# Opening stage of a decoder-layer kernel: constants in two batches, row sums taken from the rows as loaded, six token groups, and two weight tiles interleaved with the transposes

## The chip, the cores and the metric

The kernel is one launch on one core of a Trainium2 chip. The metric is the device time of that core in microseconds (us), and less is better. All arithmetic is fp32: the large products are made of TensorE's fp32r products of high and low parts, the small ones are plain fp32.

## The reference

One layer of a decoder trunk runs over 576 tokens: a prompt of 512 and eight samples of 8 tokens each. The change touches the opening of the layer, up to the first weight tiles of the first feed-forward block:

```
def rmsnorm(x, g):
    y = x * lax.rsqrt(jnp.mean(x * x, axis=-1, keepdims=True) + EPS)
    return y * g

def swiglu_ffn(x, norm_g, w_gu, w_down):
    h = rmsnorm(x, norm_g)
    g, u = jnp.split(h @ w_gu, 2, axis=-1)
    return (jax.nn.silu(g) * u) @ w_down

x = x + 0.5 * swiglu_ffn(x, norm_ffn1, ffn1_w_gu, ffn1_w_down)   # x: (576, 1024), w_gu: (1024, 5632)
...
```

After it come a projection `w_in`, a convolution branch, latent attention over the prompt and over a paged cache for the samples, a gated merge, `w_out` and a second feed-forward block of the same shape. None of these is changed.

## The kernel before, in words

**Layout.** Activations are held transposed, channels on the 128 partitions and the 576 tokens along the free axis: `xT` is eight channel tiles of 128 x 576. A product writes a unit, two PSUM banks with 288 tokens each (`halves`, `HALF`). The text counts `t` for channel tiles of x (0 to 7) and `n` for column tiles of weights; the first block has 44 of them before its down projection, gate and up in turn.

**Three products for one.** Every fp32 weight tile is split in a high part (`split_hi`, L351, ACT, a rounding copy into one of `HIS = 2` buffers) and a low part (`split_lo`, L358, POOL, four instructions, written over the raw tile in one of `RAWS = 4` buffers). `product` (L367) then does hi x hi, hi x lo and lo x hi for each of 8 channel tiles and 2 halves: 48 matmuls of 288 columns for one column tile.

**Norm.** The gain is folded into x (`x_hi`, `x_lo`); the factor 1/rms per token (`rstd`) is applied when a unit is read from PSUM (`scaled`, L1353). So the products need no norm, and only the first reading of a unit does.

**The opening, engine by engine.** ACT's queue issues 13 DMAs of constants, in this order: seven rows of gains, the convolution's taps, the identity matrix, the causal mask, the rotary table and two rows of gains broadcast (L642 to L648). All raise one semaphore, `const_in`. SP issues five DMAs for x (L440, L441) and eight for the first four weight tiles (`load_chunk`, L338), and then waits with each further tile for `w_used`. PE waits for all 13 constants (L933), transposes the gains and the taps into the columns `cols`, waits for x and transposes it, 5 transposes for each of 8 channel tiles (four of 128 tokens, one of 64), with room in PSUM for four channel tiles (L947). Only then come column tile 0, the sums, and column tiles 1, 2, 3. For each channel tile DVE copies the transposed tile to `xT` in two instructions (L1346, L1347), forms `x_lo` (L1326) and adds the squares to `sumsq` (L1333); ACT squares the tile (L656) and forms `x_hi` (L657). `sums` (L961) is three fp32 matmuls of ones with `sumsq`; DVE (`inverse`, L1335) and ACT (`rstd_root`, L659) make `rstd` of them.

**What sets the order.** Every engine has its own program, written out by hand, and counts on semaphores. What matters here of ACT's order, from `up_phase` (L692): split of column tile 2, root, split of tile 3, `hidden` for the first pair (SiLU, then the high part of the result), and only then the splits of tiles 4 and 5. `split_hi` of tile n waits for the end of tile n - 2 (`w_used`). `chunk` (L951) on PE waits for the low part of its tile. DVE's `hidden` (L1357) reads two units, multiplies by ACT's SiLU and forms the low part.

## Time and profile before

| | |
|---|---|
| Median of 3 runs | 1736.98 us (1735.47 to 1738.48) |
| Profiled execution, own time | 1737.28 us |
| Its span in the profile | 1735.5 us |
| PE busy | 1634.6 us, 94% of the span |
| DVE, POOL, ACT busy | 746.7, 608.5, 530.8 us |
| From the start to the first large matmul | 30.2 us |

A span is the time from the first to the last instruction of the trace; the execution's own time is 1.8 us longer. PE is TensorE's matmuls, PEld its loads of the stationary operand, DVE is VectorE, ACT ScalarE, POOL GpSimd, SP the queue that issues most DMAs. A name with q (SPq, ACTq) is that engine's sequencer. "issue" is a wait for nothing that the profile shows.

### The profile page before, as it was taken

How to read it: one execution, taken by the hardware profiler on the slowest of the kernel's cores; microseconds unless marked ns; L12 is line 12 of the kernel's file. 1: busy time of each engine (PE TensorE's matmuls, PEld its weight loads, DVE VectorE, ACT ScalarE, POOL GpSimd, SP SyncE). 2: the span in 40 equal slices, each digit the busy share in tenths (PEclk: the TensorE clock that was granted, in tenths of full speed). 3: DMA queues.
4: the chain of work that ended last, by engine and by line, in shares of the span. 5: the costliest groups of instructions: out<-in, count | busy, mean ns of one | idle time of the engine just before them, and what ended most of it. 6: DMA issues, size and time to landing. Idle time of an engine off the chain costs nothing.

```text
span 1735.5 us, 31195 instructions
## 1 busy us (share of the span) xinstructions
PE 1634.6 (94%) x11545; PEld 1546.3 (89%) x11545; DVE 746.7 (43%) x1147; ACT 530.8 (31%) x915; POOL 608.5 (35%) x693
## 2 busy tenths in 40 slices
PE   5999999999899999787999999978999999999998
PEld 4999999999899998375988888867999999999997
DVE  5322222121269856663666666666543222221001
ACT  3222222222121232242544444434233222222110
POOL 2455555544345544100000000002655555454441
PEclk9999999999999999897999999998999999999999
DMA  4222223322223421001212122210222222223221
GB/s 125 74 85 85 83 75 88 101 83 79 60 74 95 118 61 54 0 1 52 56 46 58 53 57 54 57 36 25 85 85 73 85 85 80 77 85 101 84 83 55
DMA packets 230060, 122.05 MB, mean 70 GB/s; under 512 B 28223, under 2 KB 226983, under 8 KB 229972
## 3 DMA queue, kind: packets, MB, share of 16 engines
q1 hardware_dynamic: 229150, 120.56, 24.4%
q8 instruction: 43, 0.70, 0.2%
q10 hardware_dynamic: 830, 0.48, 0.1%
q14 instruction: 37, 0.30, 0.1%
HBM read 117.79 MB, written 3.58 MB: 70 GB/s over the span
## 4 chain that ended last, share of the span: by engine, by line
PE 83%; DVE 6%; issue 4%; ACT 3%; POOL 2%; SPq 1%; DMA 1%; ACTq 0%; DVEq 0%; POOLq 0%
PE ps L377 61%; PE ps L1250 11%; PE ps L1197 3%; POOL w_lobuf L363 2%; PE ps L1104 1%; PE ps L1183 1%; PE ps L1071 1%; ACT prob L800 1%; PE ps L1078 1%; PE ps L1223 1%; DMA gqk<-in_q_head_norm 1%; DVE s_buf L1695 1%; DVE y L1410 1%; SPq L499 1%; SPq L500 0%
## 5 line engine op out<-in xcount | busy, mean ns | idle before, releaser
L363 POOL TENSOR_TENSOR w_lobuf<-w_rawbuf,w_hibuf 128x256 fp32r<-128x256 f32 (+1 forms) x664 | 583.9, 911 | 662.6 <-ACT w_hibuf L356 662.6
L377 PE MATMUL ps<-x_hi,w_hibuf 128*128 128x288 f32 x1888 | 408.9, 298 | 8.6 <-POOL w_lobuf L363 3.1
L377 PE MATMUL ps<-x_hi,w_lobuf 128*128 128x288 f32 x1888 | 407.4, 297 | 0.0
L377 PE MATMUL ps<-x_lo,w_hibuf 128*128 128x288 f32 x1888 | 407.0, 297 | 0.0
L356 ACT ACTIVATE w_hibuf<-w_rawbuf 128x1024 fp32r<-128x1024 f32 (+1 forms) x166 | 185.3, 1116 | 679.1 <-PE ps L377 679.1
L377 PEld LDWEIGHTS ps<-x_hi,w_hibuf 128*128 128x128 f32 x1888 | 305.1, 189 | 11.4 <-issue 4.5
L377 PEld LDWEIGHTS ps<-x_hi,w_lobuf 128*128 128x128 f32 x1888 | 305.1, 189 | 0.4
L377 PEld LDWEIGHTS ps<-x_lo,w_hibuf 128*128 128x128 f32 x1888 | 305.0, 189 | 0.4
L377 PE MATMUL ps<-a_lo,w_hibuf 128*128 128x288 f32 x704 | 151.2, 296 | 0.0
L377 PE MATMUL ps<-a_hi,w_lobuf 128*128 128x288 f32 x704 | 151.1, 296 | 0.0
L377 PE MATMUL ps<-a_hi,w_hibuf 128*128 128x288 f32 x704 | 150.9, 296 | 0.0
L1355 DVE TENSOR_TENSOR tb<-ps,rstd 128x576 f32<-128x576 f32 x48 | 36.4, 758 | 249.3 <-PE ps L377 249.3
L1250 PE MATMUL ps<-kq_hi,cT_hi 128*128 128x288 f32 x512 | 125.3, 326 | 7.7 <-DVE cT_lo L1673 7.7
L1756 DVE TENSOR_REDUCE page_ss<-sq 128x8 f32<-128x512 f32 x128 | 85.4, 681 | 101.5 <-ACT sq L872 100.9
L1384 DVE SCALAR_TENSOR_TENSOR xT<-ps,xT 128x576 f32<-128x576 f32 x24 | 18.2, 757 | 248.0 <-PE ps L377 248.0
L622 POOL TENSOR_TENSOR ta<-kpe_nat 128x512 f32<-128x512 f32 x8 | 8.4, 1054 | 312.3 <-DMA kpe_nat<-in_cache_kpe 312.3
L377 PEld LDWEIGHTS ps<-a_hi,w_lobuf 128*128 128x128 f32 x704 | 113.7, 188 | 0.0
L377 PEld LDWEIGHTS ps<-a_lo,w_hibuf 128*128 128x128 f32 x704 | 113.7, 188 | 0.0
L377 PEld LDWEIGHTS ps<-a_hi,w_hibuf 128*128 128x128 f32 x704 | 113.7, 188 | 0.0
L1250 PE MATMUL ps<-kq_hi,cT_lo 128*128 128x288 f32 x512 | 110.5, 297 | 0.0
L1250 PE MATMUL ps<-kq_lo,cT_hi 128*128 128x288 f32 x512 | 110.4, 297 | 0.0
L1410 DVE SCALAR_TENSOR_TENSOR y<-ext,cols,y 128x512 f32<-128x512 f32 x120 | 104.5, 871 | 2.6
(266 smaller groups left out, 1998.2 us busy)
## 6 DMA issues: line engine op xcount, KB each, us to landing
w_rawbuf<-in_ffn_w_gu SPq DMA_DIRECT2D x176, 256.0 KB, 3.2
c_nat<-in_cache_ckv SPq DMA_DIRECT2D x128, 128.0 KB, 2.0
w_rawbuf<-in_w_in SPq DMA_DIRECT2D x58, 256.0 KB, 3.2
w_rawbuf<-in_ffn_w_down SPq DMA_DIRECT2D x32, 384.0 KB, 3.8
w_rawbuf<-in_ffn_w_down SPq DMA_DIRECT2D x32, 320.0 KB, 3.1
w_rawbuf<-in_w_out SPq DMA_DIRECT2D x16, 256.0 KB, 3.0
x_nat<-in_x_prompt SPq DMA_DIRECT2D x4, 512.0 KB, 4.9
w_rawbuf<-in_w_conv_out SPq DMA_DIRECT2D x8, 256.0 KB, 2.9
```

The lines of the kernel that those rows point to most:

```text
L356: act.activation(w_hibuf[:, r % HIS, 0:size], w_rawbuf[:, r, 0:size], ACT.Copy).then_inc(w_hi_done, 1)
L363: ins = pool.tensor_tensor(w_lobuf[:, r, part], w_rawbuf[:, r, part], w_hibuf[:, r % HIS, part].bitcast(F32), ALU.subtract)
L377: mm = pe.matmul(ps[0:width, 2 * s + h, 0:HALF], a, b[:, k, h * HALF:(h + 1) * HALF], start=first and i == 0 and j == 0, stop=last and i = ...
L499: page = sp.value_load(pages[0:1, ds(s * NP + t, 1)], min_val=0, max_val=cache_ckv.shape[1] - 1)
L800: act.activation(prob[:, qi, 0:(qi + 1) * P], ps[:, 2 + qi, 0:(qi + 1) * P], ACT.Exp, bias=small[:, 1, qi:qi + 1], scale=SCALE, accum_out= ...
L1071: mm = pe.matmul(ps[0:n, 2 * s + b, 0:QL], qaT[k][:, i * P:i * P + n], w_uq[:, k, b * QL:(b + 1) * QL], start=k == 0, stop=k == QL // P - 1)
L1197: mm = pe.matmul(ps[0:HQ, 7, 0:KL], s_buf[:, b, t, :], c_nat[:, b, t, :], start=t == 0, stop=False)
L1250: mm = pe.matmul(ps[:, page_banks(t) + half, 0:KQ], a, m[:, half, cols], start=k == 0 and j == 0, stop=k == 1 and j == 2)
L1355: return dve.tensor_tensor(halves(dst), unit(s)[0:rows], halves(rstd[0:rows, :]), ALU.mult)
L1384: dve.scalar_tensor_tensor(x2, unit(s), scale, x2, op0=ALU.mult, op1=ALU.add).then_inc(x_done, 1)
L1410: dve.scalar_tensor_tensor(dst, src, cw, dst, op0=ALU.mult, op1=ALU.add).then_inc(conv_p_step, 1)
L1756: dve.tensor_reduce(page_ss[:, t, :], sq[:, u, 0:H * DN].rearrange("p (h d) -> p h d", d=DN), AX, ALU.add).then_inc(page_red, 1)
```

## The change

Five things are done, all ahead of the first block's main loop.

1. **Constants in two batches.** The identity goes first on ACT's queue, then the gains and taps; these nine raise `rows_in`, on which PE waits. The other four raise `const_in`, on which PE waits once the first two column tiles are done.
2. **Six token groups.** x is loaded and transposed in groups of 128, 128, 32, 128, 128 and 32 tokens, so that a group never crosses the two halves; that is 7 DMAs instead of 5 and 6 transposes per channel tile instead of 5. A channel tile is then copied by one DVE instruction over both halves, and `x_lo` reads x from PSUM. PSUM holds two channel tiles instead of four, and the transposes of tile t wait for `x_lo` of tile t - 2.
3. **Row sums.** For the first norm ACT squares each group's rows as they were loaded (`row_squares`, one activation over 1024 elements with an accumulated sum), one group ahead of the tiles and five between them. DVE and ACT turn the 128 x 6 sums into factors, DVE puts each group's on a diagonal, and eight fp32 matmuls with ones (`first_rstd`) spread them over the partitions. The sums of squares per channel tile go; the later two norms are as before.
4. **Interleaving.** Column tile 0 runs channel tile by channel tile as soon as `x_lo` of each is there, with the transposes of tile k + 2 behind it, and column tile 1 follows four channel tiles later. Their low parts are signalled by quarter (`w_piece`).
5. **Order.** `first_rstd` stands after column tile 2, where `sums` stood after column tile 0. DVE copies the result to `rstd`; before, it was in PSUM, a reciprocal and a root over 576 elements away.

```diff
+X_GROUPS = ((0, 128), (128, 128), (256, 32), (288, 128), (416, 128), (544, 32))
+NX = len(X_GROUPS)
...
-            for i in range(PT_TILES):
-                sp.dma_start(x_nat[:, i, :], x_prompt[0, i * P:(i + 1) * P, :]).then_inc(x_in, 16)
-            sp.dma_start(x_nat[0:TS, PT_TILES, :], x_sample.rearrange("s t d -> (s t) d")).then_inc(x_in, 16)
+            for g, (t0, n) in enumerate(X_GROUPS):
+                prompt = max(0, min(n, TP - t0))
+                if prompt:
+                    sp.dma_start(x_nat[0:prompt, g, :], x_prompt[0, t0:t0 + prompt, :]).then_inc(x_in, 16)
+                if prompt < n:
+                    sp.dma_start(x_nat[prompt:n, g, :], new[t0 + prompt - TP:t0 + n - TP, :]).then_inc(x_in, 16)
...
+            for n in range(2):
+                pool.wait_ge(w_hi_done, n + 1)
+                for c in range(4):
+                    part = slice(c * KD * P // 4, (c + 1) * KD * P // 4)
+                    pool.tensor_tensor(w_lobuf[:, n, part], w_rawbuf[:, n, part], w_hibuf[:, n, part].bitcast(F32), ALU.subtract)\
+                        .then_inc(w_piece, 1)
+                pool.wait_ge(w_piece, 4 * n + 4)
+                pool.sem_inc(w_lo_done, 1)
...
+            act.dma_start(ident[:, :], const["ident"]).then_inc(rows_in, 16)
...
-            act.dma_start(ident[:, :], const["ident"]).then_inc(const_in, 16)
...
+            def row_squares(g):
+                n = X_GROUPS[g][1]
+                act.activation(x_sq[0:n, :], x_nat[0:n, g, :], ACT.Square, accum_out=x_ss[0:n, g:g + 1]).then_inc(x_squared, 1)
+                act.wait_ge(x_squared, g + 1)
+
+            act.wait_ge(x_in, 7 * 16)
+            act.wait_ge(ones_done, 2)
+            row_squares(0)
             act.wait_ge(unit_read, 4)
             for t in range(KD):
-                x_parts(0, t, t, G_FFN1)
                 if t < 2:
                     split_hi(act, t, t, KD * P, free=False)
+                act.wait_ge(x_done, t + 1)
+                act.activation(x_hi[:, t, :], xT[:, t, :], ACT.Copy, scale=cols[:, G_FFN1 + t:G_FFN1 + t + 1]).then_inc(xh_done, 1)
+                if 2 <= t < NX + 1:
+                    row_squares(t - 1)
...
-                rstd_root(v)
+                if v:
+                    rstd_root(v)
+                else:
+                    act.wait_ge(x_inv, 1)
+                    act.activation(x_ss[:, :], x_ss[:, :], ACT.Sqrt).then_inc(x_root, 1)
...
-            pe.wait_ge(const_in, 13 * 16)
+            pe.wait_ge(rows_in, 9 * 16)
...
+            def x_transposes(t):
+                if t >= 2:
+                    pe.wait_ge(xl_done, t - 1)
+                for g, (t0, n) in enumerate(X_GROUPS):
+                    tr = pe.transpose(ps[:, 4 + 2 * (t % 2) + t0 // HALF, t0 % HALF:t0 % HALF + n],
+                                      x_nat[0:n, g, t * P:(t + 1) * P], ident[0:n, 0:n])
                 tr.then_inc(tr_done, 1)
+
+            def first_chunk(n, k):
+                pe.wait_ge(xl_done, k + 1)
+                pe.wait_ge(w_piece, 4 * n + k // 2 + 1)
+                mm = product(pe, n, n, range(k, k + 1), x_hi, x_lo, w0=k, first=k == 0, last=k == KD - 1)
+                if k == KD - 1:
+                    mm.then_inc(w_used, 1)
+
+            def first_pair():
+                LAG = 4
+                x_transposes(0)
+                x_transposes(1)
+                pe.wait_ge(unit_read, 4)
+                for k in range(KD):
+                    first_chunk(0, k)
+                    if k + 2 < KD:
+                        x_transposes(k + 2)
+                    if k >= LAG:
+                        first_chunk(1, k - LAG)
+                for k in range(KD - LAG, KD):
+                    first_chunk(1, k)
+                pe.wait_ge(const_in, 4 * 16)
+
+            def first_rstd():
+                pe.wait_ge(x_spread, 1)
+                pe.wait_ge(ones_done, 1)
+                third = T // 3
+                for g, (t0, n) in enumerate(X_GROUPS):
+                    for b in range(3):
+                        a, z = max(t0, b * third), min(t0 + n, (b + 1) * third)
+                        if a < z:
+                            mm = pe.matmul(stat0[:, b, a - b * third:z - b * third], ones[0:n, :], x_diag[0:n, g, a - t0:z - t0],
+                                           start=True, stop=True)
+                mm.then_inc(x_rstd, 1)
...
-                up_pair(n_up, q_up, 0, 0, x_ready(v), KD * v + KD - 3, norm=v, **x)
-                pe.wait_ge(var_done, v + 1)
-                with pe.Fori(0, FT // 2 - 1) as i:
+                if v:
+                    up_pair(n_up, q_up, 0, 0, x_ready(v), KD * v + KD - 3, norm=v, **x)
+                    pe.wait_ge(var_done, v)
+                else:
+                    first_pair()
+                    chunk(2, 2, q_up + 2, (q_up + 2) % 4, range(KD), x_hi, x_lo)
+                    first_rstd()
+                    chunk(3, 3, q_up + 3, (q_up + 3) % 4, range(KD), x_hi, x_lo)
+                    up_pair(n_up, q_up, 2, 0, **x)
+                with pe.Fori(0 if v else 1, FT // 2 - 1) as i:
...
             for t in range(KD):
+                xs = ps[:, 4 + 2 * (t % 2):6 + 2 * (t % 2), 0:HALF]
                 dve.wait_ge(tr_done, t + 2)
-                dve.tensor_copy(xT[:, t, 0:TP], ps[:, 2 * (t % 4), :])
-                dve.tensor_copy(xT[:, t, TP:T], ps[:, 2 * (t % 4) + 1, 0:TS]).then_inc(x_done, 1)
-                if t:
-                    x_low(0, t - 1, t - 1, G_FFN1, x_hi, x_lo)
-            x_low(0, KD - 1, KD - 1, G_FFN1, x_hi, x_lo)
-            inverse(0)
+                dve.tensor_copy(halves(xT[:, t, :]), xs).then_inc(x_done, 1)
+                dve.wait_ge(xh_done, t + 1)
+                dve.scalar_tensor_tensor(halves(x_lo[:, t, :]), xs, cols[:, G_FFN1 + t:G_FFN1 + t + 1],
+                                         halves(x_hi[:, t, :]).bitcast(F32), op0=ALU.mult, op1=ALU.subtract).then_inc(xl_done, 1)
+            dve.wait_ge(x_squared, NX)
+            dve.tensor_scalar(x_ss[:, :], x_ss[:, :], 1.0 / D, EPS, ALU.mult, ALU.add).then_inc(x_var, 1)
+            dve.wait_ge(x_var, 1)
+            dve.reciprocal(x_ss[:, :], x_ss[:, :]).then_inc(x_inv, 1)
+            dve.wait_ge(x_root, 1)
+            for g in range(NX):
+                n = X_GROUPS[g][1]
+                ins = dve.tensor_scalar(x_diag[0:n, g, 0:n], ident[0:n, 0:n], x_ss[0:n, g:g + 1], None, ALU.mult)
+            ins.then_inc(x_spread, 1)
+            dve.wait_ge(x_rstd, 1)
+            dve.tensor_copy(rstd[:, :].rearrange("p (b n) -> p b n", b=3), stat0).then_inc(rstd_done, 1)
```

## Rows read from the trace of the kernel before

**Rows 1.** Page, chain that ended last: shares of the span by engine.
```profile
PE 83%; DVE 6%; issue 4%; ACT 3%; POOL 2%; SPq 1%; DMA 1%; ACTq 0%; DVEq 0%; POOLq 0%
```
**Rows 2.** Busy time by 10 us: PE, PEld, DVE, ACT, POOL, clock, DMA, GB/s.
```profile
30.00:40.00 10.00, 8.45 (x49) 8.01 (x50) 9.66 (x16) 5.42 (x8) 0.51 (x1) 1.00 0.00 0
```
**Rows 3.** Chain of waits, opening, in order of time: start, duration, what.
```profile
5.83 10.07 DMA gqk<-in_q_head_norm
...
38.19 0.83 DVE x_lo L1326
...
40.13 0.97 PE ps L966 x6
41.10 20.93 PE ps L377 x157
```
**Rows 4.** Timeline, DMA issues of SP: start, duration, engine, line, operation.
```profile
3.27 12.89 SPq L345 DMA_DIRECT2D w_rawbuf<-in_ffn_w_gu  x8
```
**Rows 5.** DMA view, 12 to 16 us: queue of the constants, packets, MB, share.
```profile
q10 hardware_dynamic: 52, 0.03, 2.8%
```
**Rows 6.** One tile's view, w_rawbuf, first 60 us: DMA issue to landing.
```profile
DMA to landing us min/median/max: 3.0/4.7/11.7
```
**Rows 7.** Timeline of DVE and ACT, one channel tile, and one x_lo beside POOL.
```profile
29.89 1.23 DVE L1326 SCALAR_TENSOR_TENSOR x_lo<-xT,cols,x_hi 128x576 fp32r<-128x576 f32 x1
...
33.84 0.68 DVE L1346 COPY xT<-ps 128x512 f32<-128x512 f32 x1
34.44 0.21 DVE L1347 COPY xT<-ps 128x64 f32<-128x64 f32 x1
34.57 0.81 DVE L1326 SCALAR_TENSOR_TENSOR x_lo<-xT,cols,x_hi 128x576 fp32r<-128x576 f32 x1
35.27 0.77 ACT L657 ACTIVATE x_hi<-xT,cols 128x576 fp32r<-128x576 f32 x1
35.96 0.68 DVE L1346 COPY xT<-ps 128x512 f32<-128x512 f32 x1
```
**Rows 8.** Groups by line and shape: busy, mean ns, idle before.
```profile
L356 ACT ACTIVATE w_hibuf<-w_rawbuf 128x1024 fp32r<-128x1024 f32 x133 | 140.7, 1058 | 471.6 <-PE ps L377 471.6
L1355 DVE TENSOR_TENSOR tb<-ps,rstd 128x576 f32<-128x576 f32 x48 | 36.4, 758 | 249.3 <-PE ps L377 249.3
L757 ACT ACTIVATION_READ_ACCUMULATOR sq<-lat 128x1 f32 x4 | 0.7, 186 | 0.0
```
**Rows 9.** Timeline, PE: transposes, and pairs of large matmuls.
```profile
16.76 9.45 PE L947 MATMUL ps<-ident,x_nat 128*128 128x128 f32 x35
19.14 1.01 PEld L947 LDWEIGHTS ps<-ident,x_nat 64*128 64x128 f32 x5 [0.33 <-issue]
20.48 1.01 PEld L947 LDWEIGHTS ps<-ident,x_nat 64*128 64x128 f32 x5 [0.33 <-issue]
...
31.81 0.68 PE L377 MATMUL ps<-x_hi,w_hibuf 128*128 128x288 f32 x2
32.29 0.68 PE L377 MATMUL ps<-x_lo,w_hibuf 128*128 128x288 f32 x2
...
60.14 0.43 PE L377 MATMUL ps<-x_hi,w_hibuf 128*128 128x288 f32 x2
```
**Rows 10.** Timeline, PE's loads in a later stretch of transposes.
```profile
615.78 0.70 PEld L1047 LDWEIGHTS ps<-ident,latT 32*128 32x128 f32 x6 [0.17 <-issue]
616.65 0.70 PEld L1047 LDWEIGHTS ps<-ident,latT 32*128 32x128 f32 x6 [0.17 <-issue]
```
**Rows 11.** Timeline, ACT and POOL from 40 us.
```profile
40.23 1.06 ACT L356 ACTIVATE w_hibuf<-w_rawbuf 128x1024 fp32r<-128x1024 f32 x1 [2.07 <-PE ps L377]
41.36 2.83 POOL L363 TENSOR_TENSOR w_lobuf<-w_rawbuf,w_hibuf 128x256 fp32r<-128x256 f32 x4 [10.86 <-ACT w_hibuf L356]
```
**Rows 12.** Busy time of PE and granted clock around a later stretch of transposes.
```profile
797.90:801.40 3.50, 3.34 (x17) 0.51 0.33 88
801.40:804.80 3.40, 1.72 (x16) 1.00 0.42 121
```

More of the change, by code:

```diff
@@ L240, in layer @@
         stat = ps[:, 5:8, HALF:HALF + T // 3]
-        const_in = sem("const_in")
+        stat0 = ps[:, 0:3, HALF:HALF + T // 3]
+        rows_in, const_in = sem("rows_in"), sem("const_in")
+        w_piece = sem("w_piece")
+        x_squared, x_var, x_inv, x_root, x_spread, x_rstd = (
+            sem(n) for n in ("x_squared", "x_var", "x_inv", "x_root", "x_spread", "x_rstd"))
         x_in = sem("x_in")
@@ L548, in _ @@
             pool.memset(ones[:, :], 1.0).then_inc(ones_done, 1)
+            pool.memset(x_ss[:, :], 1.0).then_inc(ones_done, 1)
             def lo4(n, n0, size):
@@ L552, in lo4 @@
                     split_lo(pool, n + g, (n0 + g) % RAWS, size)
-            with pool.Fori(0, FT // 2) as i:
+            for n in range(2):
[6 more added lines that the diff above has]
+                pool.sem_inc(w_lo_done, 1)
+            for n in range(2, 4):
+                split_lo(pool, n, n, KD * P)
+            with pool.Fori(1, FT // 2) as i:
                 lo4(i * 4 + n_ffn1_up, n_ffn1_up, KD * P)
@@ L641, in _ @@
                                  ("q_a_norm", G_QA, QL // P)):
[L642 to L644 removed]
+                act.dma_start(gain_rows[row:row + k, :], w[name][0].rearrange("(k p) -> k p", p=P)).then_inc(rows_in, 16)
+            act.dma_start(conv_rows[:, :], w["conv_w"][0]).then_inc(rows_in, 16)
             act.dma_start(causal[:, :], const["causal"]).then_inc(const_in, 16)
@@ L652, in x_parts @@
                 act.wait_ge(x_done, t + (KD * v + 1))
-                if v or not isinstance(t, int) or t >= 2:
-                    act.wait_ge(acc_done, t + (KD * v - 1))
+                if v > 1 or t >= 2:
+                    act.wait_ge(acc_done, t + (KD * (v - 1) - 1))
                 tile = xT[:, ds(t, 1), :]
@@ L937, in _ @@
             tr.then_inc(tr_done, 1)
-            pe.wait_ge(x_in, 80)
-            for t in range(KD):
-                if t == 3:
-                    pe.wait_ge(unit_read, 4)
-                if t >= 4:
-                    pe.wait_ge(x_done, t - 3)
-                for i in range(NT):
-                    n = P if i < PT_TILES else TS
-                    c = (i % PT_TILES) * P
-                    tr = pe.transpose(ps[:, 2 * (t % 4) + i // PT_TILES, c:c + n],
-                                      x_nat[0:n, i, t * P:(t + 1) * P], ident[0:n, 0:n])
-                tr.then_inc(tr_done, 1)
+            pe.wait_ge(x_in, 7 * 16)
@@ L1186, in soft_pe @@
             def soft_pe(r, b):
-                pe.wait_ge(const_in, 13 * 16)
+                pe.wait_ge(rows_in, 9 * 16)
                 pe.wait_ge(max_done, r + 1)
@@ L1205, in soft_pe @@
                 yield
-                pe.wait_ge(const_in, 13 * 16)
+                pe.wait_ge(rows_in, 9 * 16)
                 pe.wait_ge(lat_scaled, r + 1)
```

35 lines of the change are left out of this document (19 added, 16 removed).

## The prediction

> **What bounds the kernel now.** I read the page's chain first: PE holds 83% of it, DVE 6% [rows 1]. Over the whole span only PE's stream counts, so I looked for the place where that stream becomes unbroken. The busy time by stage puts it at 40 us: from 30 to 40 us DVE is busy 9.66 of 10 us and PE 8.45, and the clock column says 1.00 there although the first matmuls are at half rate (below) [rows 2]. The chain of waits in order of time shows three stretches ahead of that: the landing of the thirteenth constant at 15.9 us, then DVE's work on x up to 38.19 + 0.83 = 39.0 us, then PE alone, with the sums at 40.13 and one run of 157 matmuls in 20.93 us, 0.1333 us each [rows 3]. From 41 us on the kernel is PE's; what the change does to the time is what it does to the moment at which PE's stream is unbroken. I take as mark the first matmul of column tile 4, at 60.14 us [rows 9]: all before it is touched by the change, nothing behind it is. Column tiles 1, 2, 3 take 3 x 48 x 0.1333 = 19.2 us before it.
>
> **Step 1, the start.** PE now waits for the first nine of 13 constants. The queue of the constants moves its last 52 packets between 12 and 16 us, 2.8% of the engines' time [rows 5], so these are the tails of the last DMAs; the ninth lands between 12 and 15.9 us, and I take 13.5, near the lower row, since the four left out come behind it. From 13.5: gains and taps take 0.85 (15.9 to the transposes at 16.76 [rows 3, 9]), six transposes at half rate 1.5. That comes from 1.34 us for five (19.14 to 20.48 [rows 9]) plus a second short group, which costs a break of about 0.16. So the first channel tile can be copied at 15.95 and is in xT at 16.7. The weights do not come earlier: SP holds its eight issues over 12.89 us since the queue is full, so two more DMAs for x ahead of them hide in that [rows 4], and the second half of column tile 0, issued near 3.9, lands at 11.7 behind it, 15.6 [rows 6]. ACT has split it at 15.6 + 1.06 [rows 8]. Two paths meet at 16.7; x_hi and x_lo of channel tile 0 are done at 18.3. SP issues a half tile every 12.89 / 8 = 1.6 us, so column tile 1 lands some 1.6 us behind, at 17.2; so its split stands ahead of the second x_hi, at 17.4 to 18.4, beside the copy. x_lo 1 is done at 20.6.
>
> **Step 2, the rhythm per channel tile.** Before it was 33.84 to 35.96 = 2.12 us of DVE, two copies, x_lo and the sum [rows 7]; while POOL ran, x_lo took 1.23 instead of 0.81. Now copy, x_hi and x_lo follow each other, since DVE waits for ACT inside the tile: a copy from PSUM 0.76 (as the 576-wide read of PSUM, [rows 8]), ACT 0.77 less overlap, x_lo 0.77, 0.03 for each hand-over, and 0.07 of overlap back: 2.29 us. Gone is the sum (0.75), come is the wait. x_lo reads PSUM, and so escapes POOL, I reckon (0.76, by the same row). ACT has in that time x_hi 0.67, a row square of 1024 elements 1.06 [rows 8], its accumulator 0.19 [rows 8] and a wait for itself, 0.1: 2.0, under 2.29, so it hides; bare of that cover it would cost up to 1.3 per tile.
>
> PE has its own rhythm, because the transposes of tile k + 2 stand behind column tile 0's six matmuls of k, and PSUM holds two tiles. At half rate six matmuls are 6 x 0.24 [rows 9] + 0.15 for the change from transposes = 1.59, transposes 1.50: 3.09, over DVE's 2.29. At full rate six matmuls take 6 x 0.1333 + 0.13 = 0.93, transposes 1.05 (six in 0.87 with one short group [rows 10], a second for one long: +0.2), together 1.98, under it. From k = 4 column tile 1's six come on top: 4.53 or 2.78. So the time hangs on PE's clock, whose cost I bound from both sides:
> - full rate from the first matmul: last x_lo at 34.6, both column tiles done at 39.5;
> - half rate until 26 us: 36.8 and 41.7; until 30 us: 37.8 and 42.7; until 34 us: 39.6 and 44.5; until 38 us: 40.7 and 45.6.
>
> Each is the recurrence: x_lo(k+2) = the later of x_lo(k+1) + 2.29 and end of transposes(k+2) + 2.4, then 0.93 + 5 x 0.8 = 4.9 us of matmuls behind the last. Before, the opening's transposes ran at half rate for 9.45 us, with their breaks of 0.33 [rows 9], and the large matmuls, begun at 30.2, were still 0.24 apart at 31.81 to 32.29 [rows 9] and 0.133 in the run of [rows 3]. The new mix is denser than those transposes (1.44 us of matmuls in 3.09), and denser again from k = 4, at 31 us. I take 28 us: last x_lo 37.4, pair done 42.2.
>
> **Step 3, column tile 2.** Its high part waits for the end of column tile 0 (HIS = 2), which now is only 4.0 us before that of tile 1. Split 1.06, POOL 2.83, hand-overs 0.4 [rows 11]: 4.3, so PE waits 0.3. Before, this had 7.2 us to hide in. It runs from 42.5 to 49.05. Column tile 3 has the time of tile 2 as cover.
>
> **Step 4, first_rstd.** Before, the sums took 0.97 by the chain [rows 3], 0.84 from start to start. Now 576 columns are spread on eight products, with three changes between 128 and 32 rows; at 0.97 for the columns and 0.15 for each change, 1.4 us, bounds 0.97 and 2.5. PE: 50.45, and column tile 3 runs to 57.0. The 3.75 us reciprocal and the wide root of before are gone, but they lay beside matmuls.
>
> **Step 5, a new wait.** ACT splits column tile 4 only after the first pair's SiLU and high part, and these now wait for first_rstd. From its end: copy to rstd 0.2 + 0.76, loop set-up 0.25, reading the gate unit 0.76, SiLU 0.7, product 0.1 + 0.76, high part 0.7, split 1.06, POOL 2.83, hand-overs 0.2: 8.3 us, against 6.5 for column tile 3. PE waits 1.75 us, once; behind the late split stand tile 5's on ACT and POOL, which have column tile 4 as cover. Column tile 4 begins at 58.8, against 60.14. Taking copy and unit read at nothing would leave 0.2, so the price lies between 0.2 and 3.
>
> **Costed at nothing.** Six diagonals on DVE (some 2 us) and the small root lie beside column tile 2, 6.5 us. The late `const_in` is 26 us past its landing. POOL's second memset (0.2) and `sem_inc` have idle time to 16.6 us. Without that cover each costs its own length.
>
> **Sum.** 60.14 - 58.8 = 1.4 us less. The span goes from 1735.5 to 1734.1, the profiled execution's own time from 1737.28 to 1735.9; the median of the runs shown is 0.3 under that execution, so 1735.6.
>
> **A rule of the Trainium skill.** At 797.9 to 801.4 us PE did sixteen transposes almost without a break at a granted 0.51, and the next stretch has 1.00 [rows 12]; at the opening 9.45 us of them did not bring it [rows 9]. TensorE: Matmul & The Clock Gate, section PE-mode transpose, says that the full clock does not engage for transposes, as they don't count as PE-busy in the same way. The trace agrees at the opening and disagrees at 801 us. By that rule the opening would go as in rival A.
>
> **The rivals.**
> - **A, slower: the half rate stays.** Place: channel tiles 2 to 7. If the transposes between them keep PE at 1.2 GHz through k = 7, each step from k = 4 costs 4.53, column tile 0 ends at 44.2, and column tile 1's last matmuls at 49.5 if the rate rises at 46: column tile 4 begins at 65.7, 5.6 us late, 1742.6. Breaking even lies near a rise at 32.5 us. For it: the 9.45 us at half rate. Against: matmuls fill half and more of the time.
> - **B, clearly faster.** The rate is full by 20 us or so, or step 5's wait is half of mine: 3.1 to 5.9 us less, 1731 to 1734. For it: idle between 17.5 and 18.3 is short. Against: large matmuls begin only at 18.4.
> - **C, the constants are no lever.** If the ninth lands at 15.9 as the thirteenth did, all shifts by 2.4 us: 1 us slower than before, 1738. For it: one queue feeds all. Against: the causal mask, rotary table and broadcasts no longer stand before.
> - **D, the rhythm is ACT's.** If a row square blocks ACT for over 1.6 us, five tiles gain 0.3 each: 1737.
>
> **How the numbers follow.** Forecast 0.45, A 0.15, B 0.25, C 0.08, D 0.07. A difference of 0.2%, 3.5 us, is about what can be told from none here. B crosses it in most of its range, 0.22, and the forecast at its end, 0.02: faster 0.24. A crosses it in three quarters of its range, 0.12, C with a late rate 0.03: slower 0.15. Within it is the rest, 0.61. For 8 in 10 I leave out the end of A and of B: 1731.5 to 1740.5. The forecast's own range is 1733.5 to 1737.
>
> **What would show it.** First transposes at about 13.5 + 0.85 (step 1; C if 16.8). x_lo starts 2.3 us apart or 3.1 (step 2), with 0.24 or 0.133 us between matmuls. The first matmul of column tile 2 0.3 behind column tile 1's last (step 3). 1.4 us of fp32 matmuls behind column tile 2. PE idle 1.75 us before column tile 4, released by POOL's low part (step 5). Column tile 4 near 58.8. The prediction is wrong if that mark moved by something else, or if a stretch beyond 60 us changed its length.

## The result and the profile after

The changed kernel took 1743.03 us (median of 17 runs, 1740.48 to 1746.42), the kernel before 1737.74 (17 runs). The ratio is 1.0034, with a 95% interval from 1.0026 to 1.0041: slower by 5.3 us. That is small, but the interval is clear of 1, and the time lies outside the predicted range. The profiled execution had a span of 1739.0 us against 1735.5.

The timeline of PE in the opening, with start and length of each group in us. The second number of a pair of large matmuls is 0.68 where the two stand 0.24 us apart, and 0.43 where they stand 0.133 apart. 0.24 us is the half rate, PE's clock at the lower of its two levels (1.2 GHz): in a_warm, below, the granted clock is on record for 18 to 26 us as 0.50, and its matmuls are 0.24 apart there. "Rate" always means this level.

```profile
14.49 0.32 PE L977 MATMUL ps<-ident,gain_rows 39*128 39x39 f32 x1 [14.49 <-DMA conv_rows<-in_conv_w]
...
19.72 0.82 PE L389 MATMUL ps<-x_hi,w_hibuf 128*128 128x288 f32 x2 [0.91 <-DVE x_lo L1434]
20.34 0.68 PE L389 MATMUL ps<-x_lo,w_hibuf 128*128 128x288 f32 x2
20.82 0.68 PE L389 MATMUL ps<-x_hi,w_lobuf 128*128 128x288 f32 x2
21.30 1.73 PE L988 MATMUL ps<-ident,x_nat 128*128 128x128 f32 x6
22.96 0.85 PE L389 MATMUL ps<-x_hi,w_hibuf 128*128 128x288 f32 x2
...
37.63 0.68 PE L389 MATMUL ps<-x_hi,w_hibuf 128*128 128x288 f32 x2
...
39.07 1.60 PE L988 MATMUL ps<-ident,x_nat 128*128 128x128 f32 x6
40.60 0.54 PE L389 MATMUL ps<-x_hi,w_hibuf 128*128 128x288 f32 x2
40.98 0.43 PE L389 MATMUL ps<-x_lo,w_hibuf 128*128 128x288 f32 x2
```

PE begins at 14.49 us, 1.46 earlier than the 15.95 of before. Then it is almost never idle and yet slow: six matmuls and six transposes take 22.96 - 19.72 = 3.24 us, and the matmuls are 0.24 us apart until about 40 us. At 40.98 they are 0.133 apart. The kernel before had the same low rate at 31.81 and 32.29 [rows 9], 1.6 us after its first large matmul, and went over to 0.133 at about 33.4.

The chain of waits of the changed kernel (start, length, what):

```profile
4.10 10.35 DMA conv_rows<-in_conv_w
...
31.30 1.53 PE ps L988 x6
32.83 1.74 PE ps L389 x6
34.56 1.53 PE ps L988 x6
36.09 3.18 PE ps L389 x12
39.27 1.40 PE ps L988 x6
40.67 3.65 PE ps L389 x24
...
44.41 1.07 ACT w_hibuf L368
...
62.41 2.80 POOL w_lobuf L375 x4
65.21 0.04 issue
65.25 0.81 PE ps L389 x4
```

From 19.7 to 44.3 us the chain is PE alone, where before it was DVE's work on x up to 39.0 us [rows 3]. So the change did take DVE off the path, and put PE, most of that time at half rate, in its place.

The mark of the prediction, the first matmul of column tile 4, is at 65.25 us against 60.14 [rows 9], 5.11 later. Where the 5.11 us arise is read from three places: the first matmul of column tile 2 (before, then after), the small matmuls behind that tile, and the wait ahead of column tile 4.

```profile
47.34 0.43 PE L377 MATMUL ps<-x_hi,w_hibuf 128*128 128x288 f32 x2
```
```profile
48.48 0.51 PE L389 MATMUL ps<-x_hi,w_hibuf 128*128 128x288 f32 x2 [0.16 <-issue]
...
54.95 2.31 PE L1025 MATMUL ps<-x_diag,ones 128*128 128x128 f32 x16
...
65.25 0.54 PE L389 MATMUL ps<-x_hi,w_hibuf 128*128 128x288 f32 x2 [1.40 <-POOL w_lobuf L375]
```

Column tile 2 begins 1.14 us later than before, where the forecast, with 42.5, had it 4.8 us earlier. The small matmuls take 2.24 us (54.95 to 57.19) at a place where the kernel before had none, since its sums are already in the 47.34. PE then loses 1.56 us ahead of column tile 4, and the two column tiles themselves 0.17. So two costs that the prediction knew, 3.8 us together, had to be paid out of what the opening was to gain ahead of column tile 2, and the opening gained nothing.

Behind the mark the distance stays at 5.22 up to 435 us. That the spans end only 3.5 apart comes of several stretches at half rate whose place or length differs between these two executions. The clearest is at 528 us: the kernel before had one there, and this execution of the changed kernel had none, though PE had waited about 2 us for POOL just ahead in both (the matmul behind the wait, before and after; then start and end of the stretch, its length, PE, PEld, DVE, ACT, POOL busy, the clock, DMA share and GB/s, before and after):

```profile
527.68 0.54 PE L377 MATMUL ps<-x_hi,w_hibuf 128*128 128x288 f32 x2 [2.06 <-POOL w_lobuf L363]
```
```profile
533.65 0.53 PE L389 MATMUL ps<-x_hi,w_hibuf 128*128 128x288 f32 x2 [2.07 <-POOL w_lobuf L375]
```

```profile
528.00:532.00 4.00, 4.00 (x21) 4.00 (x20) 3.89 (x4) 0.00 (x0) 3.73 (x4) 0.57 0.19 57
```
```profile
528.00:532.00 4.00, 3.58 (x27) 3.34 (x26) 3.96 (x5) 1.09 (x2) 3.16 (x2) 1.00 0.09 28
```

The distance is 5.97 at 527.68 and 533.65, and 4.45 once that stretch is over; it comes down to 3.5 between 560 and 650 us.

The wait ahead of column tile 4 has the cause that step 5 named: DVE's copy of the root follows the small matmuls, and ACT can split column tile 4 only when the first pair's work behind that copy is done.

```profile
57.30 0.76 DVE L1446 COPY rstd<-ps 128x576 f32<-128x576 f32 x1 [8.16 <-PE ps L1025]
```
```profile
61.27 1.05 ACT L368 ACTIVATE w_hibuf<-w_rawbuf 128x1024 fp32r<-128x1024 f32 x1
```

### The profile page after: what moved, and what is told of

It is laid out like the page before. It is cut to its first block, busy times and chain, and to the rows that moved or that the text cites. A ratio compares the mean times of both kernels' runs of the same rounds, so it can differ in the third digit from the quotient of the medians.

```text
span 1739.0 us, 31203 instructions
## 1 busy us (share of the span) xinstructions
PE 1640.9 (94%) x11563; PEld 1549.8 (89%) x11563; DVE 736.3 (42%) x1138; ACT 532.3 (31%) x919; POOL 603.6 (35%) x694
## 4 chain that ended last, share of the span: by engine, by line
PE 83%; DVE 5%; issue 4%; ACT 2%; POOL 2%; SPq 1%; DMA 1%; ACTq 0%; DVEq 0%; POOLq 0%
PE ps L389 60%; PE ps L1335 11%; PE ps L1282 3%; POOL w_lobuf L375 2%; PE ps L1189 1%; PE ps L1268 1%; PE ps L1156 1%; ACT prob L843 1%; PE ps L1163 1%; PE ps L1308 1%; PE ps L988 1%; DMA conv_rows<-in_conv_w 1%; DVE s_buf L1790 1%; DVE y L1505 1%; SPq L515 1%
## 5 line engine op out<-in xcount | busy, mean ns | idle before, releaser
L375 POOL TENSOR_TENSOR w_lobuf<-w_rawbuf,w_hibuf 128x256 fp32r<-128x256 f32 (+2 forms) x656 | 573.4, 906 | 654.9 <-ACT w_hibuf L368 654.9
```

Source lines behind the costliest of these rows:

```text
L375: ins = pool.tensor_tensor(w_lobuf[:, r, part], w_rawbuf[:, r, part], w_hibuf[:, r % HIS, part].bitcast(F32), ALU.subtract)
```

## The experiments

Two theories. **H**: the change loses because its matmuls now stand in the stretch in which PE is at half rate, and its stream keeps that rate for long. **R**: the hand-over between DVE and ACT, with PSUM room for two channel tiles, sets the pace, and PE's rate only follows. "The mark" is the first matmul of column tile 4 in the profiled execution; "rise" is where large matmuls go over from 0.24 to 0.133 us apart. Both come from one execution each. How far a rise can differ between executions, the table itself shows: the change, a_warm and a_split4 give PE the same instructions from its first large matmul to the rise, and it came at 40.3, 38.4 and 39.9; so do a_order and c_best, and 25.6 in one stands against 22.8 and 36.5 in the other.

| kernel | time, us | ratio to before [95%] | rise | mark |
|---|---|---|---|---|
| before | 1737.5 | 1 | 33.4 | 60.14 |
| the change | 1743.03 | 1.0034 [1.0026, 1.0041] | 40.3 | 65.25 |
| a_warm | 1742.63 | 1.0029 [1.0018, 1.0040] | 38.4 | 64.16 |
| a_lag1 | 1743.40 | 1.0040 [1.0027, 1.0054] | 28.9 | 64.41 |
| a_lag8 | 1744.08 | 1.0040 [1.0026, 1.0053] | 46.6 | 67.98 |
| a_fill | 1742.02 | 1.0024 [1.0015, 1.0033] | 31.3 | 63.46 |
| a_order | 1736.07 | 0.9993 [0.9984, 1.0002] | 25.6 | 59.21 |
| a_split4 | 1740.73 | 1.0022 [1.0013, 1.0031] | 39.9 | 63.56 |
| a_plain | 1741.75 | 1.0027 [1.0016, 1.0038] | 36.6 | 64.24 |
| c_best | 1734.54 | 0.9986 [0.9977, 0.9995] | 22.8, 36.5 | 59.65 |
| b_rows | 1734.62 | 0.9986 [0.9977, 0.9995] | 30.0 | 57.16 |
| b_batches | 1735.24 | 0.9987 [0.9978, 0.9996] | 32.1 | 57.86 |
| d_both | 1733.22 | 0.9979 [0.9969, 0.9989] | 29.3 | 55.81 |
| d_best | 1730.82 | 0.9964 [0.9950, 0.9977] | 28.2 | 54.37 |

The time given for the kernel before is the median of 33 runs taken beside a_fill, c_best, b_rows and b_batches; beside the others it was 1736.55 to 1737.74, so small differences are read from the ratios and marks.

**a_warm: PE is busy before its first wait.**

```diff
+            pe.wait_ge(ones_done, 1)
+            for _ in range(48):
+                pe.matmul(ps[:, 0, 0:P], ones[:, :], ones[:, :], start=True, stop=True)
             pe.wait_ge(rows_in, 9 * 16)
```

> The changed kernel with 48 fp32 matmuls of ones with ones in front of PE's first wait, so that PE works through the time in which it idles for the constants (to 14.5 us). Theory H (the half rate costs it): the matmuls of the interleaved stage come 0.133 apart instead of 0.24, x_lo 2.4 us apart instead of 3.27, column tile 4 begins near 59 instead of 65.25, and the time falls by 5 to 7 us, to 1736 to 1738, at or below the kernel before. Rival R (the hand-overs between DVE and ACT and PSUM's room for two tiles cost it, whatever the rate): x_lo stays 3.2 us apart, under 1 us gained. A third outcome: the rate is up at 15 us and falls again during the transposes; then the stage goes as in the changed kernel and the rule that transposes don't hold the clock has its case.

The third outcome came: the rate was full for the first transposes and gone for the first matmul.

```profile
14.97 2.24 PE L991 MATMUL ps<-ident,x_nat 128*128 128x128 f32 x12
19.19 0.82 PE L389 MATMUL ps<-x_hi,w_hibuf 128*128 128x288 f32 x2 [1.97 <-DVE x_lo L1437]
19.81 0.68 PE L389 MATMUL ps<-x_lo,w_hibuf 128*128 128x288 f32 x2
```

Twelve transposes in 2.24 us (3.51 at half rate), then a wait of 1.97 us for x_lo, and matmuls 0.24 apart. The run tells nothing for or against H: the full rate was lost before it was needed. The mark came 1.09 us earlier, but the time is no different from that of the change.

**a_lag1, a_lag8: column tile 1 beside or behind the transposes.** `LAG = 1` and `LAG = 8` in place of 4.

> The changed kernel with LAG = 1: column tile 1 follows one channel tile behind column tile 0 instead of four, so the matmuls are 12 to 6 transposes from the second channel tile on, not from the fifth. If what PE does between the transposes decides when its rate rises (H): the rise comes near 28 to 31 us instead of 40.3, and the time falls by 2 to 4 us. If the half rate is held by the transposes as such, the stage runs at 4.9 us per channel tile to the end, x_lo 7 comes near 50 instead of 43, and it is 3 to 6 us slower.

> The changed kernel with LAG 8 in place of 4: column tile 0 is interleaved with the transposes as before, column tile 1 comes wholly behind it, so that 24 of its 48 matmuls move out of the transposes' stretch. H: those of them that stood ahead of the rise were paid at 0.24 us there, and the rate rises about 3 us after the last transposes in either case (with the transposes ending near 39.3 at a period of 3.27, near 42.5). Then of the 60 matmuls left some 13 are at 0.24 and 47 at 0.133: pair done near 48.7 against 48.2, column tile 4 near 65.8 against 65.25, 1743.5, no difference that can be measured. R (matmuls beside the transposes are covered by the hand-over of VectorE and ScalarE): 24 matmuls more behind the transposes, 3.2 us: column tile 4 at 68.5, 1746.2.

The more matmuls stood beside the transposes, the earlier the rise: 28.9 us with LAG 1, 40.3 with 4, 46.6 with 8. R has no reason for that. H's forecast of the time for LAG 1, 2 to 4 us less, did not come: 1743.40 against 1743.03. The gain was given back at once: column tiles 0 and 1 now end together, at about 43.6 instead of 48.2 us, so nothing covers the split of column tile 2 (ACT at 42.2, POOL up to about 46.1), PE is idle for 2.51 us, and the matmuls behind the wait are 0.24 apart again.

```profile
43.29 0.43 PE L389 MATMUL ps<-x_hi,w_lobuf 128*128 128x288 f32 x2
46.23 0.82 PE L389 MATMUL ps<-x_hi,w_hibuf 128*128 128x288 f32 x2 [2.51 <-issue]
46.85 0.68 PE L389 MATMUL ps<-x_lo,w_hibuf 128*128 128x288 f32 x2
...
49.58 0.43 PE L389 MATMUL ps<-x_lo,w_hibuf 128*128 128x288 f32 x2
```

LAG 8 put the mark at 67.98, nearer R's 68.5 than H's 65.8. My number took the rise about 3 us behind the last transposes, near 42.5; it came at 46.6, 7.3 us behind them, after a wait of 0.83 us at 41.95. The median, 1744.08, is nearer H's 1743.5 than R's 1746.2. Taken by itself, this run doesn't decide between the two: that the matmuls are still 0.24 apart at 45.96 is neither theory's number.

**a_fill: more work for PE, none taken away.**

```diff
                         x_transposes(k + 2)
+                    if k in (1, 2):
+                        for _ in range(6):
+                            pe.matmul(ps[:, 3, 0:HALF], w_hibuf[:, 0, 0:P], x_hi[:, 0, 0:HALF], start=True, stop=True)
```

> The changed kernel, with twelve more matmuls of 128 columns by 288 rows' width on TensorE (six behind the transposes of chunk 3, six behind those of chunk 4 of column tile 0), written to a PSUM bank that nothing reads before it is overwritten. Transposes, their order, LAG and everything else as in the change, so this is work added and none taken away. Theory H (the change lost because TensorE stood at half rate until 40.3 us, and the rate rises sooner where more of its stream is plain matmuls): the rate rises near 29 us, as with LAG 1; the last x_lo of the opening near 38 instead of 42.4, the pair of column tiles done near 44 instead of 48.2, the first matmul of column tile 4 near 61 instead of 65.2, the kernel near 1739, 4 us under the change, although it computes 12 matmuls more. Theory R (the rhythm of VectorE and ScalarE's hand-over with the PSUM room of two tiles sets the opening, and the rate only follows it): TensorE has 2.9 us more to do at 0.24 us each, and all ends are later: pair done near 51, column tile 4 near 68, 1746.

```profile
26.61 1.81 PE L1012 MATMUL ps<-x_hi,w_hibuf 128*128 128x288 f32 x6
...
29.65 1.73 PE L988 MATMUL ps<-ident,x_nat 128*128 128x128 f32 x6
31.31 1.06 PE L1012 MATMUL ps<-x_hi,w_hibuf 128*128 128x288 f32 x6
32.21 0.43 PE L389 MATMUL ps<-x_hi,w_hibuf 128*128 128x288 f32 x2
```

Six useless matmuls took 1.81 us the first time and 1.06 the second: the rate rose between, 9 us sooner than in the change. The mark came 1.8 us earlier although PE had 12 matmuls more. That speaks for H, and plainly against R, which asked for 68 and 1746 us. The size was less than the 4 us expected: the rise was at 31.3 and not at 29, the median only 1.0 us under that of the change, and the two intervals overlap. So the run excludes R's loss; a gain it shows in one trace alone.

**a_order: the four groups of 128 tokens, then the two of 32.**

```diff
-                for g, (t0, n) in enumerate(X_GROUPS):
+                for g in (0, 1, 3, 4, 2, 5):
+                    t0, n = X_GROUPS[g]
                     tr = pe.transpose(ps[:, 4 + 2 * (t % 2) + t0 // HALF, t0 % HALF:t0 % HALF + n],
```

> The changed kernel with the four transposes of 128 tokens first and the two of 32 behind them, so that PE changes between 128 and 32 rows twice per channel tile and not four times. H: transposes take 1.3 us instead of 1.67 at half rate, six steps of 0.35 us: 2 us less for the last x_lo, and the mix is denser, so the rate may rise one stage earlier (then 3 to 4 us less). R, with the rhythm set by DVE and ACT: no change, since their chain is 2.4 us per tile in any case.

```profile
20.73 1.40 PE L989 MATMUL ps<-ident,x_nat 128*128 128x128 f32 x6
22.07 0.85 PE L389 MATMUL ps<-x_hi,w_hibuf 128*128 128x288 f32 x2
...
25.92 0.42 PE L389 MATMUL ps<-x_hi,w_lobuf 128*128 128x288 f32 x2
26.18 0.83 PE L989 MATMUL ps<-ident,x_nat 128*128 128x128 f32 x6
27.65 0.54 PE L389 MATMUL ps<-x_hi,w_hibuf 128*128 128x288 f32 x2 [0.63 <-DVE x_lo L1435]
```

The same six transposes take 22.07 - 20.73 = 1.34 us instead of 1.66 (21.30 to 22.96): each time the number of rows goes from 128 to 32 and back, PE loses about 0.3 us, and the order of the change does so once more per channel tile. And the rise comes at 25.6 instead of 40.3, with nothing else altered. The mark is 6 us earlier, the median 7, where R expected no change. Column tile 2 begins at 42.44 us, the 42.5 of the forecast: this is the opening that the prediction had in mind, and it shows what the late rise cost. The edit does two things at once, shorter transposes (eight times 0.3 us) and the earlier rise; about half of the 6 us or more is left for the rise. Behind the rise PE waits 0.63 us for x_lo at two channel tiles, and x_lo come 2.4 us apart: there R's pace is the limit, as the prediction's 2.29. So R names the floor, and H what stood 0.85 us above it in the change (x_lo 3.26 apart).

**a_split4: the wait ahead of column tile 4.**

```diff
                 second_pair_hi(v, n0)
+                if v == 0:
+                    split_hi(act, n0 + 4, 0, KD * P)
                 hidden(f, q0, 0, a_hi)
```

(tile 5's split follows that hidden tile, and the loop begins one later.)

> The changed kernel with ACT's split of column tile 4 ahead of the first pair's SiLU and high part instead of behind them (tile 5's behind the first high part). All theories: POOL's low part of tile 4 is done by 60, PE's wait of 1.4 us before column tile 4 goes. If that wait is on the path that sets the end, the time falls by 1.4 us; if PE would wait elsewhere for the same chain (the first unit must be read before column tile 4 can write it), by under 0.5.

No gap is left ahead of column tile 4, and the mark is 1.69 us earlier, the median 2.3. So the wait was on the path, whatever PE's rate in the opening.

**a_plain: the interleaving alone undone.**

```diff
-                LAG = 4
-                x_transposes(0)
-                x_transposes(1)
+                for k in range(KD):
+                    x_transposes(k)
                 pe.wait_ge(unit_read, 4)
-                for k in range(KD):
-                    first_chunk(0, k)
-                    if k + 2 < KD:
-                        x_transposes(k + 2)
-                    if k >= LAG:
-                        first_chunk(1, k - LAG)
-                for k in range(KD - LAG, KD):
-                    first_chunk(1, k)
+                for n in range(2):
+                    for k in range(KD):
+                        first_chunk(n, k)
```

> The changed kernel with its interleaving alone undone: TensorE issues all eight chunks' transposes first (PSUM room for two chunks, so that chunk t waits for x_lo of t-2, as in the change), then column tile 0, then column tile 1. Theory H, in the form that the runs so far give it: TensorE is at half rate during the transposes in either order; interleaved, the matmuls of the column tiles are paid at 0.24 us there, behind them they meet a rate that rises 2.5 to 3.5 us after the first of them. In the kernel with row squares alone the two column tiles took 13.9 us from first to last. All transposes issued near 32.5, pair done near 46.4 against 48.2, column tile 4 near 63.3 against 65.25: 1741, 2 us under the change although no multiplication lies beside the transposes any more. Theory R (the interleaving gains, and something else of the change loses): undoing it costs what it covered, at least 16 plain matmuls' time: column tile 4 at 67 or later, 1745 or more.

No multiplication stands beside the transposes any more, and the mark is 1.0 us earlier, the median 1.3 (the two intervals overlap): as the change has it, interleaving costs at least what it covers. But it is only 1.0 of the 5.11 us. The mark is still 4.1 us later than before, of which 3.8 are the small matmuls and the wait ahead of column tile 4, as in the change; column tile 2 begins at 47.54, level with the 47.34 of before. Why it isn't earlier, though the constants landed 1.6 us sooner and DVE has less to do, is in the waits of PE, whole opening, first for this kernel, then for b_rows (what waits, for what: us in total, times, longest):

```profile
PE ps L988 <- DVE x_lo L1428: 3.7, 6, 0.9
```
```profile
PE ps L382 <- DVE rstd L1402: 1.2, 1, 1.2
```

With room for two channel tiles in PSUM, and x_lo straight behind its own copy on DVE, each set of transposes waits for an x_lo, six times 0.6 us, and the first large matmul comes at 33.1 us. With four tiles of room, and x_lo one tile behind the copies, b_rows has no such wait, and its first comes at 27.5. That is R's part of the loss. A kernel with the change's interleaving and PSUM room for four tiles was not run.

**b_rows, b_batches, d_both: parts of the change in the kernel before.** b_rows takes the squares from the rows as loaded, with five groups, PE's order as before, and the small matmuls behind column tile 1; b_batches only the order and the two waits of the constants (the second one stands behind the first two column tiles, not behind the transposes as the expectation says); d_both has both.

```diff
             for t in range(KD):
-                x_parts(0, t, t, G_FFN1)
+                act.wait_ge(x_done, t + 1)
+                act.activation(x_hi[:, t, :], xT[:, t, :], ACT.Copy, scale=cols[:, G_FFN1 + t:G_FFN1 + t + 1]).then_inc(xh_done, 1)
...
+                if 3 <= t < NT + 2:
+                    row_squares(t - 2)
```

> The kernel before with one part of the change alone: the squares summed from the rows as loaded, five row groups as it has them, the root spread by small matmuls of a diagonal behind column tile 1; constants, the order of TensorE's work and the transposes as before. VectorE no longer adds a tile of squares (0.77 of its 2.29 us per chunk) and ScalarE no longer squares it (1.06). H: this part is worth its 0.6 to 0.7 us a chunk over those chunks for which TensorE waits (x_lo at 38.2 near 34.5), and TensorE's one wait of the opening before the last matmuls of column tile 0 shrinks; nothing of it is given back, since TensorE's stream is as before: 3 us less at the start of column tile 4 (57 against 60.1), 1734.5. R: as far as the hand-over sets the opening it gains the same, 3 us: the two theories agree here, and the run only shows what this part is worth without the interleaving. Third outcome: TensorE is held by its own half rate in column tile 0, and the gain is under 1 us.

```diff
-            pe.wait_ge(const_in, 13 * 16)
+            pe.wait_ge(rows_in, 9 * 16)
```

> The kernel before with the other part alone: the nine constants that the first transposes need are loaded and awaited ahead, the other four are awaited behind column tile 0's transposes. In the changed kernel the first transposes ran at 14.5 us, against 15.9 before. If the start of the chain is worth its time: all marks 1.4 us earlier, column tile 4 at 58.7 instead of 60.1, 1736.1 us, ratio 0.9992. If the rows of x (landing near 16) hold the transposes anyway: under 0.3 us, ratio 1.000.

> The kernel before with the row squares and the two batches of constants, and nothing else of the change: five groups, transposes for four chunks ahead, no interleaving. Alone they moved the start of column tile 4 by 2.98 and 2.28 us. H (each acts on the same chain at its own place, its start and its rhythm, so they add): column tile 4 at 54.9 against 60.1, 1732.3 us, ratio 0.997. If one of them only removed waiting that the other leaves elsewhere: 56 to 57, 1734.

Each part gains by itself: the mark moves by 2.98, by 2.28, and by 4.33 with both. The nine constants land at 13.67 us in b_batches, 14.03 in d_both, 14.49 in the change and 14.88 in a_fill, against 15.95 before, so this part is worth 1.1 to 2.3 us from one execution to the next, and the marks of b_rows and b_batches don't quite add. The x_lo of b_rows begin 1.7 us apart on average (20.3 to 32.2), against 2.3 before. d_both came out 0.9 us over its expectation in both the mark and the median.

**c_best, d_best: two ways to a faster kernel.** c_best is the change with the edits of a_order and a_split4, and the small matmuls in the same order. d_best is d_both with the small matmuls behind column tile 2, into banks 0 to 2, and the edit of a_split4; its main edit is this:

```diff
-                    sums(0)
-                    pe.wait_ge(rstd_done, 1)
+                    chunk(2, 2, q_up + 2, (q_up + 2) % 4, range(KD), x_hi, x_lo)
+                    sums(0)
+                    chunk(3, 3, q_up + 3, (q_up + 3) % 4, range(KD), x_hi, x_lo)
+                    up_pair(n_up, q_up, 2, 0, **x)
```

> The changed kernel with three edits together: the transposes of a chunk in the order 0, 1, 3, 4, 2, 5 (the four groups of 128 tokens, then the two of 32), the 14 small matmuls that spread the root over the partitions in the same order, and ScalarE's split of the weights of column tile 4 ahead of its first hidden tile. H: the first two give what the order alone gave (the rate rises near 25.6 us, column tile 2 starts near 42.4), the third takes away the 1.57 us gap ahead of column tile 4, which then starts near 57.5 instead of 59.2 (57.2 if the small matmuls too are quicker in that order: 1.9 us instead of 2.24). 1734.3 us, 0.998 of the kernel before, its interval below 1. R: the gain of the order would be all that the hand-over allows, and the gap ahead of column tile 4 is off the path that ends last: 1736, no different from the order alone.

> As the last one, with the small matmuls that spread the root moved behind column tile 2 into banks 0 to 2 (as the change has them), and ScalarE's split of column tile 4 ahead of its first hidden tile. In the kernel with row squares alone TensorE waited 1.44 us behind the small matmuls for VectorE's copy of the root out of the banks of column tile 2; here that wait lies beside column tile 3, and the gap of 1.57 ahead of column tile 4 doesn't come. Column tile 4 at 53.5, 1731.0 us, ratio 0.9963. If the wait only moves (to the split of a later column tile): no better than the last one, 1732.3.

c_best reached 1734.54, as expected (1734.3), though not in its profiled execution (1737.36, mark 59.65 against the 57.5 expected): in that one the rate rose at 22.8, fell at 29.7 while PE waited 0.65 us per channel tile, and rose again at 36.5.

```profile
28.16 0.83 PE L996 MATMUL ps<-ident,x_nat 128*128 128x128 f32 x6
29.64 0.85 PE L389 MATMUL ps<-x_hi,w_hibuf 128*128 128x288 f32 x2 [0.65 <-DVE x_lo L1443]
30.28 0.68 PE L389 MATMUL ps<-x_lo,w_hibuf 128*128 128x288 f32 x2
```

d_best is the fastest: 1730.82 us (1731.0 expected), 0.9964 of the kernel before [0.9950, 0.9977], 12 us under the change. Its mark, 54.37, came 0.9 us later than the 53.5 expected. Its chain of waits is whole:

```profile
4.37 10.07 DMA conv_rows<-in_conv_w
14.43 0.04 issue
14.48 0.33 PE ps L964
14.80 0.56 PE ps L966 x4
15.36 10.72 PE ps L977 x40
26.09 20.37 PE ps L383 x144
46.45 1.48 PE ps L1001 x12
47.93 12.20 PE ps L383 x90
```

From the landing of the constants to 60 us, where the view ends, PE waits for nothing. Its 40 transposes take 10.72 us at half rate (10.79 in b_rows), and of the large matmuls only those of the first 2.2 us are 0.24 apart.

## Why the prediction was wrong

The step that failed is step 2, in the sentence "I take 28 us" for the moment at which PE's rate rises. It rose at 40.3. What a late rise would do was told rightly: PE's rhythm at half rate over DVE's, 3.09 against 2.29 forecast, 3.26 against 2.38 measured. Rival A, held at 0.15, came nearest: column tile 4 at 65.7 and 1742.6 us, measured 65.25 and 1743.0. That its numbers fit so well is in part luck. It had the half rate hold through the last channel tile, to 46 us; it ended at 40.3, and the 1.3 us of step 1, the longer transposes and the 0.84 us of step 4 made up the difference.

- **Step 1.** Forecast: x_lo 0 done at 18.3. Measured: it begins at 18.80, done at 19.6. The ninth constant landed at 14.49 and not at 13.5, column tile 0's second half at 16.7 and not at 15.6: the two more DMAs for x did not hide, SP's eight issues of weights began at 4.22 instead of 3.27 [rows 4] and took as long as before. (That a full queue holds SP is shown by no row; the rows show only how long its issues take.) 1.3 us of the error. Rival C fell: b_batches gains 2.28.
- **Step 2.** Forecast: a channel tile in 3.09 us at half rate, both column tiles done at 42.2. Measured: 3.26 us, and 48.2. Transposes took 1.66 and not 1.50, since the sixth group stands between two of 128 and costs two changes of rows; I had counted one break of 0.16. The rest is the rise. Step 1 and this together make 6.0 of the 6.45 us by which the mark missed 58.8. DVE's pace was right: forecast 2.29, measured 2.38 in a_plain, where PE didn't set it. That x_lo from PSUM would escape POOL was right too: 0.82 us beside it at 21.13. Rival D fell with that: a row square took ACT 1.04 us and its accumulator 0.19, and x_lo stayed 2.38 apart.
- **Step 3.** Forecast: PE waits 0.3 before column tile 2. Measured: 48.02 to 48.48 us, 0.33 over the usual spacing.
- **Step 4.** Forecast 1.4 us, bounds 0.97 and 2.5; measured 2.24 (54.95 to 57.19). Mis-sized by 0.84. The changes of rows were sized about right: in the other order, with one instead of three, it took 1.99 (c_best), 0.12 for each. What grew was the 0.97 for the columns: the same 576 columns take 0.84 in three products (before), 1.57 in six (d_best) and 1.99 in eight.
- **Step 5.** Forecast: 8.3 us from the small matmuls to column tile 4, of which PE waits 1.75. Measured: 8.1 (57.19 to 65.25) and 1.56. a_split4 shows that it was on the path.
- **The time beyond the mark.** The sum went by one execution. The changed kernel's runs spread over 6 us (1740.48 to 1746.42), and the profiled one, 1741.14, was among its lowest; it missed its forecast of 1735.9 by 5.2 us, the median its 1735.6 by 7.4. The record has the mean granted clock of each run: 0.978 in the eight shortest (up to 1742.71), 0.976 in the nine longest (from 1743.03). The profiled one has 0.978. Longer runs thus stood longer at half rate: 0.002 of 1740 us is, at half the rate, about 7 us more of it, which costs at most 3.5 us (an estimate). The traces of a_fill and a_split4, both at 0.976, do have the stretch near 530 us that this one lacks. Why one execution has it and another not stays open.

Why the estimate of the rise was wrong can be said: I argued that matmuls fill half of the new mix, more than in the opening of before, where transposes alone kept PE at 1.2 GHz for 9.45 us [rows 9]. The mix was denser, and the rate stayed at half for 20 us all the same. The rule of the Trainium skill that I weighed (TensorE: Matmul & The Clock Gate, section PE-mode transpose: the full clock does not engage for transposes) would have given rival A. The runs agree with it in the change (six transposes between every six matmuls, 20 us at 0.24 apart) and in its direction in a_lag1 and a_fill; against it as a strict rule stand a_order, where the rate rose with as many transposes in the stream, and the 16 transposes at 797.9 us [rows 12].

What I missed besides is what the half rate cost before: little. In the kernel before, the transposes ran ahead at half rate while DVE was the slower (PE waited 0.73 and 1.88 us for its copies), and the large matmuls came behind in one block, of which only the first 3 us were slow. The change moved the two into one another, so that every matmul and every transpose of that stretch was on PE's path, at the half rate's price. The steps of the prediction added up the pieces at either rate; they did not ask in which of the two orders PE's slow time has cover. a_plain bounds this, though: with the order undone and all else kept, 1.0 us comes back at the mark, because the room for two channel tiles then holds the transposes up instead.

## What to carry to other kernels

Before moving multiplications into a stretch where PE is still at its low rate, ask what that rate costs where it is: transposes that run ahead of a slower engine pay little for it (before), matmuls put between them pay in full (the change), and once the other engine is faster the transposes pay too (d_best, 10.72 us). Edits with separate effects should be timed one by one: two parts of this change gain 3.0 and 2.3 us at the mark, and what else it does, the six groups with room for two, the interleaving and the new places of the small matmuls and of the wait, took both and 5 us more. Order transposes of unequal row counts so that equal ones are neighbours.

## What the runs showed of the hardware

- A change between 128 and 32 rows in a row of transposes costs PE about 0.3 us per channel tile at half rate (1.66 against 1.34 us for six), and still 0.27 at full rate (1.03 in a_lag1, 29.17 to 30.20, against 0.76 in a_order, 30.95 to 31.71).
- 576 columns spread by small fp32 matmuls took PE 0.84 us in three products, 1.57 in six (46.29 to 47.86 in d_best) and 1.99 in eight (51.15 to 53.14 in c_best), all at full rate.
- The same transposes in another order came with a rise of PE's clock at 25.6 us instead of 40.3, twelve extra matmuls with one at 31.3; one trace each. The order alone doesn't fix it: c_best, with the same order, rose at 22.8, fell at 29.7 and rose again at 36.5.
- PE stood at half rate behind a wait of 1.97 us in a_warm and of 2.51 in a_lag1. In the kernel before it fell to it within 0.7 us behind a wait of 2.06 (527.68), and in the change it kept the full rate behind the same wait of 2.07 (533.65). In c_best waits of 0.6 us per channel tile preceded a fall, in a_order with such waits the rate held. So the length of one wait doesn't tell what follows.
- The clock column is not to be trusted in an opening: at 16 to 40 us it says 1.00 for the changed kernel, where the matmuls stand 0.24 us apart, and 0.50 at 20 to 36 us for a_warm, whose matmuls are as far apart. There the spacing of equal matmuls is the clock.
